# Attention outputs come out transposed: values as the stationary operand, probabilities scaled before their transposition, gates z turned by VectorE's blocks and DRAM

## What is computed

```python
proj = einsum('bsd,de->bse', rms_norm(x), w_in)
qa, ka, va, za, qb, kb, vb, zb, qm, zm, gates = split(proj)
ya = moba_attention(rope(qa), rope(ka), va) * silu(za)      # 8 heads of 128, causal
yb = dilated_mixture(rope(qb), rope(kb), vb) * silu(zb)     # 4 output heads of 128, 3 groups each
ym = memory_attention(qm, mk, mv) * silu(zm)                # 4 heads of 256, over 256 memory rows
g_a, g_b, g_m = split(sigmoid(gates))
merged = g_a * (ya @ w_proj_a) + g_b * (yb @ w_proj_b) + g_m * (ym @ w_proj_m)
x = x + merged @ w_out
```

## Time and profile before

| | |
|---|---|
| runs | 2193.51, 2194.4 and 2196.37 us; median 2194.4 |
| profiled execution | span 2190.4 us from the first to the last instruction; the profile gives no other time for it |
| busy | PE 99%, PEld 82%, DVE 60%, ACT 47%, POOL 7% of the span |
| DMA | mean busy share 0.69, 214 GB/s |
| units | 192 to 731 us of the span |

### The profile page before, as it was taken

The page is one execution under the profiler, slowest core; times in us unless marked ns, Lnnn a source line. Parts: engine busy times, 40 slices in busy tenths (PEclk is TensorE's granted clock), DMA queues, the critical chain, the costliest instruction groups (busy, mean ns, idle before and its releaser), DMA issues.

```text
span 2190.4 us, 25672 instructions
## 1 busy us (share of the span) xinstructions
PE 2177.8 (99%) x9870; PEld 1806.4 (82%) x9870; DVE 1323.6 (60%) x1608; ACT 1029.2 (47%) x1241; POOL 154.3 (7%) x260
## 2 busy tenths in 40 slices
PE   9999999999999999999999999999999999999998
PEld 7788888888888888888888888888888888888887
DVE  5865656676455646545676878665555555554444
ACT  6544444444444444444545666454444444444443
POOL 0010101011000000000111100120001000100000
PEclk9999999999999999999999999999999999999999
DMA  8676656577754657668878756687777777776654
GB/s 302 206 234 176 203 172 208 184 231 238 206 163 149 209 180 229 198 206 285 260 240 284 230 183 200 196 267 230 219 211 225 216 211 212 226 229 203 193 193 154
DMA packets 229731, 468.89 MB, mean 214 GB/s; under 512 B 16632, under 2 KB 16896, under 8 KB 228736
## 3 DMA queue, kind: packets, MB, share of 16 engines
q1 hardware_dynamic: 212128, 409.00, 60.4%
q0 software_dynamic: 17056, 57.69, 8.7%
q10 hardware_dynamic: 448, 0.86, 0.1%
HBM read 439.69 MB, written 27.79 MB: 213 GB/s over the span
## 4 chain that ended last, share of the span: by engine, by line
PE 97%; DVE 2%; DMA 0%; ACT 0%; issue 0%; ACTq 0%; DVEq 0%
PE ps L1549 31%; PE ps L1551 31%; PE ps L1550 31%; PE ps L1448 1%; PE ps L1470 1%; DVE w_lo L916 1%; DVE ps L1266 1%; PE ps L1417 1%; PE ps L1459 0%; DMA raw<-in_w_in 0%; PE ps L1582 0%; PE ps L1583 0%; PE ps L1581 0%; PE ps L1487 0%; PE ps L1519 0%
## 5 line engine op out<-in xcount | busy, mean ns | idle before, releaser
L916 DVE TENSOR_TENSOR w_lo<-raw,w_hi 128x1024 fp32r<-128x1024 f32 (+1 forms) x776 | 931.8, 1211 | 730.4 <-ACT w_hi L605 729.2
L605 ACT ACTIVATE w_hi<-raw 128x1024 fp32r<-128x1024 f32 (+1 forms) x776 | 811.2, 1050 | 910.9 <-PE ps L1551 836.5
L1549 PE MATMUL ps<-w_hi,xT_hi 128*128 128x512 f32 x1088 | 429.8, 395 | 0.0
L1551 PE MATMUL ps<-w_hi,xT_lo 128*128 128x512 f32 x1088 | 424.1, 390 | 0.0
L1550 PE MATMUL ps<-w_lo,xT_hi 128*128 128x512 f32 x1088 | 423.6, 389 | 0.0
L1549 PE MATMUL ps<-w_hi,u2T_hi 128*128 128x512 f32 x704 | 273.9, 389 | 0.0
L1550 PE MATMUL ps<-w_lo,u2T_hi 128*128 128x512 f32 x704 | 273.9, 389 | 0.0
L1551 PE MATMUL ps<-w_hi,u2T_lo 128*128 128x512 f32 x704 | 273.9, 389 | 0.0
L1551 PEld LDWEIGHTS ps<-w_hi,xT_lo 128*128 128x128 f32 x1088 | 204.2, 188 | 43.2
L1550 PEld LDWEIGHTS ps<-w_lo,xT_hi 128*128 128x128 f32 x1088 | 204.5, 188 | 41.0
L1549 PEld LDWEIGHTS ps<-w_hi,xT_hi 128*128 128x128 f32 x1088 | 204.4, 188 | 41.1 <-issue 0.6
(11 more groups left out here) (260 smaller groups left out, 2288.4 us busy)
## 6 DMA issues: line engine op xcount, KB each, us to landing
raw<-in_w_in SPq DMA_DIRECT2D x368, 512.0 KB, 4.4
raw<-in_w_ffn_gate SPq DMA_DIRECT2D x88, 512.0 KB, 4.4
raw<-in_w_ffn_up SPq DMA_DIRECT2D x88, 512.0 KB, 4.6
raw<-in_w_ffn_down SPq DMA_DIRECT2D x88, 512.0 KB, 4.7
raw<-in_w_out SPq DMA_DIRECT2D x64, 512.0 KB, 5.8
bounce<-tmp POOLq DMA_DIRECT2D x45, 512.0 KB, 3.4
stage<-bounce POOLq DMA_DIRECT2D x140, 128.0 KB, 5.2
raw<-in_w_mem_kv SPq DMA_DIRECT2D x32, 512.0 KB, 5.3
```

What stands on the lines that cost most here:

```text
L605: nc.scalar.activation(w_hi[:, s, 0:per], raw[:, s, 0:per], ACT.Copy).then_inc(hi_ready, 1)
L916: nc.vector.tensor_tensor(w_lo[:, s, 0:per], raw[:, s, 0:per], w_hi[:, s, 0:per].bitcast(F32), ALU.subtract)\
L1549: nc.tensor.matmul(bank(2 * par + t), x_hi, w_hi[:, s, k], start=first, stop=False)
L1551: ins = nc.tensor.matmul(bank(2 * par + t), x_lo, w_hi[:, s, k], start=False, stop=last)
```

## The change

Every unit's output now comes out of TensorE already transposed:
- `unit_values` has the values as the stationary operand and the turned probabilities moving. As the tokens are now columns of the output, the factor of a token (reciprocal of its sum times the norm's factor) can't be applied to it there, so a new step of VectorE, `unit_scale`, applies it to the exponentials in `scores` before they are turned. `unit_turn` waits for it (`u_scaled`) and stands behind chunk 3 in place of 2.
- The transposes of `y_tok` are gone. `unit_y` is now VectorE's: one product of the output in PSUM with the gate z. It, `unit_hi` and `unit_lo` run in the tile behind the unit's (behind splits 4 and 5), and the parts are made from `y_tok` in place of PSUM.
- The gates z must then be transposed too (`zmT`, `zaT`, `zbT`): the new kind of post `siluT` writes the tanh and the product into `stage`, turns 32x32 blocks and takes a trip through DRAM, five of them. The numbers of all later trips go up by five. The tile of zb comes ahead of those of vb.
- `unit_scores` takes the blocks of keys of one query block in one matmul of up to 256 columns. Each unit's probabilities are copied by one instruction.
- The steps are now hooks at a chunk (`place`), run last in their chunk. The dilated units start behind chunk 4 of tiles 21 to 24, and these tiles no longer count as tiles with a unit; the tiles 4 to 15 still do.

The core of the diff:

```diff
+        def units_in_tiles():
+            out_ = [(4 + n, 0, mem_unit(n)) for n in range(4)]
+            out_ += [(8 + n, 0, moba_unit(n)) for n in range(8)]
+            return out_ + [(21 + n, 4, dil_unit(n)) for n in range(4)]
...
             def unit_scores(unit):
-                u = w.n["u"]
-                if u:
-                    pe.wait_ge(u_lo, u)
...
-                    for (qs, ks, _), kt in unit["blocks"][t]:
+                    for qs, ks, _ in [src for src, kt in blocks if kt == 0]:
...
-                            ins = nc.tensor.matmul(ps[:, o:o + P], qT[:, qc, t * P:(t + 1) * P], kT[:, kc, kt * P:(kt + 1) * P],
+                            ins = nc.tensor.matmul(ps[:, o:o + kts * P], qT[:, qc, t * P:(t + 1) * P], kT[:, kc, 0:kts * P],
...
             def unit_turn(unit):
-                pe.wait_ge(u_exp, w("u", 1))
+                pe.wait_ge(u_scaled, unit["n"] + 1)
...
             def unit_values(unit):
-                pe.wait_ge(u_pTc, w("u", 1))
+                pe.wait_ge(u_probs, unit["n"] + 1)
+                if unit["n"]:
+                    pe.wait_ge(u_y, unit["n"])
...
+                for d in range(unit["width"] // P):
+                    for n, ((_, _, v), kt, p0, a, b) in enumerate(unit["values"]):
+                        o = unit["o_at"] + d * S
+                        ins = nc.tensor.matmul(ps[:, o + a:o + b], v(kt)[:, d * P:(d + 1) * P], probsT[:, p0:p0 + b - a],
...
-            def unit_y(unit):
-                pe.wait_ge(u_y, w("u", 1))
-                transposes(lambda t, c: y_tok[:, t, c * P:(c + 1) * P], unit["y_at"], unit["width"] // P).then_inc(u_yT, 1)
...
+                place(tiles, "pe_hooks", i, o, lambda unit=unit: unit_scores(unit))
+                place(tiles, "pe_hooks", i, o + 3, lambda unit=unit: unit_turn(unit))
+                place(tiles, "pe_hooks", i, o + (7 if o else 6), lambda unit=unit: unit_values(unit))
...
+            def unit_probs(unit):
+                act.wait_ge(u_turned, unit["n"] + 1)
...
+                place(tiles, "act_hooks", i, o + 4, lambda unit=unit: unit_exp(unit))
+                place(tiles, "act_hooks", i, o + 6, lambda unit=unit: unit_probs(unit))
+                place(tiles, "act_hooks", i, o + 13, lambda unit=unit: unit_hi(unit))
...
-            def unit_norm(unit):
-                dve.wait_ge(u_exp, w("u", 1))
+            def unit_scale(unit):
+                dve.wait_ge(u_exp, unit["n"] + 1)
                 link(nc.vector.reciprocal(rinv, rowsum))
                 link(nc.vector.tensor_tensor(rinv, rinv, R["x"]["r"], ALU.mult))
...
+                    a, n = sb_at(unit, t)
+                    ins = nc.vector.tensor_scalar(scores[:, a:a + n], scores[:, a:a + n], rinv[:, t:t + 1], None, ALU.mult)
+                ins.then_inc(u_scaled, 1)
...
+            def unit_y(unit):
+                dve.wait_ge(b_used, unit["z_turned"])
+                dve.wait_ge(u_out, unit["n"] + 1)
...
+                nc.vector.tensor_tensor(y_tok[:, 0:n], ps[:, o:o + n * S].rearrange("p (c s) -> p c s", s=S), unit["zT"],
+                                        ALU.mult).then_inc(u_y, 1)
...
+                if kind[0] == "siluT":
+                    dve.wait_ge(acc_free[par], w(f"a{par}", 1))
...
-                    if unit and unit_chunk(tile, h) == 4:
-                        unit_mask(unit)
                     if h == pos(tile, tile.get("post_at", 5 if unit else 4 if prev and prev["post"][0] == "res" and prev["post"][3] == "u" else 3)):
                         post(prev, h + 1)
...
                     for f in dict(hooks).get(h, ()):
                         f()
-                if unit and unit_chunk(tile, h) == 7:
-                    unit_norm(unit)
-                    unit_lo(unit)
...
+                place(tiles, "dve_hooks", i, o + 4, lambda unit=unit: unit_mask(unit))
+                place(tiles, "dve_hooks", i, o + 5, lambda unit=unit: unit_scale(unit))
+                place(tiles, "dve_hooks", i, o + 12, lambda unit=unit: unit_y(unit))
+                place(tiles, "dve_hooks", i, o + 13, lambda unit=unit: unit_lo(unit))
```

More of the change, by code:

```diff
@@ L396, in tiles_out @@
             three, four = res_tiles(w_out, "m", x1, 1, what="u")
-            return cut_pair([one, two, far(three, 20), far(four, 21)], 19)
+            return cut_pair([one, two, far(three, 25), far(four, 26)], 24)
         def merge_last(n):
@@ L408, in late_in @@
                 return 2
-            return 9 if len(chunks(tile)) > 9 else 3 if late and (late[0][1] or late[0][0][0] in ("res", "turn") or late[0][0][0] == "rope" and late[0][0][-1] == "late") else 1
+            return 9 if len(chunks(tile)) > 9 else 3 if late and (late[0][1] or late[0][0][0] in ("res", "turn", "siluT") or late[0][0][0] == "rope" and late[0][0][-1] == "late") else 1
         def ffn_last(n):
@@ L434, in tiles_out2 @@
             three, four = res_tiles(w_out2, "y2", h2, 1, what="u2")
-            one, two, three, four = far(one, None), far(two, 31), far(three, 32), far(four, 33)
+            one, two, three, four = far(one, None), far(two, 36), far(three, 37), far(four, 38)
             return [cut(one, 0, 0, 6, True), cut(two, 1, 0, 6, False), cut(one, 0, 6, 7, False), cut(two, 1, 6, 7, False),
@@ new lines, in unit_turn @@
+                for b, k in enumerate(unit["order"]):
+                    o = unit["p_at"] + k * P
+                    ins = nc.tensor.transpose(ps[:, o:o + P], scores[:, b * P:(b + 1) * P], ident)
+                ins.then_inc(u_turned, 1)
+            def unit_values(unit):
+                pe.wait_ge(u_probs, unit["n"] + 1)
+                if unit["n"]:
+                    pe.wait_ge(u_y, unit["n"])
+                if unit["n"] == 3 * QUAD:
+                    pe.wait_ge(acc_free[1], w("a1"))
+                for d in range(unit["width"] // P):
+                    for n, ((_, _, v), kt, p0, a, b) in enumerate(unit["values"]):
+                        o = unit["o_at"] + d * S
+                        ins = nc.tensor.matmul(ps[:, o + a:o + b], v(kt)[:, d * P:(d + 1) * P], probsT[:, p0:p0 + b - a],
+                                               start=n == 0, stop=n == len(unit["values"]) - 1)
@@ L1553, in run @@
                     w.step("g")
-                    if unit and unit_chunk(tile, h) in at_:
-                        (unit_scores, unit_turn, unit_values, unit_y)[at_.index(unit_chunk(tile, h))](unit)
                     if "ret" in tile and h == 0:
```

194 lines of the change are left out of this document (83 added, 111 removed).

## The result

The changed kernel takes 2248.1 us (median of 4 runs, 2245.4 to 2253.8) against 2194.0 for the kernel before on the same chip: a ratio of 1.0253, with a 95% interval of 1.0241 to 1.0266. That is 54 us slower; the forecast was 2234 in a range of 2217 to 2256.

What follows compares the result with a forecast made beforehand. TensorE, busy 99% of the span at 2.4 GHz, was taken as the bound. Waits of 45.4 us less 5.7 us of removed work and waits gave +39.7 us on the 2194.4 median: 2234 us, range 2217 to 2256.

Steps and rivals of the forecast that it cites:

- The waits: TensorE at unit_turn waits for VectorE's unit_scale, queued behind post, unit_y and unit_lo: 15 waits, 45.4 us in all.
- The work removed: On TensorE, y_tok transposes and short waits go and wider matmuls save time: 5.7 us less (5 to 7.5).
- The clock: TensorE's granted clock: a 2.1 us wait left it at the upper level, so no time was added for a fall.
- The forecast's own case: TensorE waits at the turns with the clock up: 2234 us, own range 2217 to 2243, chance 79%.
- the rival's 2256: TensorE's clock falls in eight waits over 3 us, one chunk each at the lower level: +22 us, 2256; chance 10%.
- Two of the signs: In the changed kernel's profile: TensorE's busy time should fall by 5 us; a granted clock leaving its level refutes the forecast.
- What lies beside: Gate z trips through DRAM, POOL's queue, ScalarE's extra copies and raw loads: all covered, adding nothing.
- six chunks or 16 us: ScalarE takes a gate z trip's result that long after the block transposes, against 8.6 us of landings and issues between.
- The three chunks (8.2 us): If a DRAM trip were late and ScalarE's next split waited, TensorE would still have this much matmul work in hand.
- No waits: VectorE's post is through before TensorE reaches the turn, only the transposes are gone: 2189, faster; chance 6%.
- A second wait per tile: ScalarE's late split 7 or VectorE's late split 6 stops TensorE again, 1 to 2 us in twelve tiles: near 2250; 5%.
- Part of the waits only: unit_y, unit_lo and scalings covered or cheaper, 0.7 to 1.4 us off twelve sums: 2217 to 2225; no separate chance given.

Runs made afterwards that it cites:

- the kernel without stops: Changed kernel with post at chunk 3, turn at chunk 5, unit_y and unit_lo behind mask and scaling, dilated units' turn one chunk later: 2185.3 us, ratio 0.9966.
- the two combined edits: Changed kernel with the post at chunk 3 and the memory and MoBA units' turn at chunk 5: 2190.0 us, ratio 0.999.

## Why the prediction came out as it did

**The waits: right, place by place.** The order that it rests on, the hooks last in their chunk and the post in front of them, stands in VectorE's timeline above. Between starts (idle time and 0.16) against the sums: MoBA units under a rotation 4.95 each, 5.0 predicted; memory units under one 3.9, 4.0 predicted; under a gate z 0.8, 3.0 and 2.5, where 0.6, 3.1 and 2.6 were predicted; dilated 0.7 and three of 1.4, as predicted; tile 7 none, as predicted. Only tile 11 is off, 0.4 for 1.1. In all 44.0 for 45.4. The unseen term, scaling of 128 columns, was taken as 0.55 for the pair from the rows of `h2`, and measured 0.55.

**The work removed: a little small.** 5.7 was taken in a range of 5 to 7.5; the difference above gives 6.8, the kernel without stops 5.5 of busy time and 7.8 in the medians. Its parts, the transposes of `y_tok`, the short waits and the wider matmuls, were not measured one by one.

**The clock: the step that failed.** The forecast's own case ended at 2243, and 2248.1 lies above it; the stated range holds it only because its upper end was drawn at the rival's 2256. Two of the signs that the prediction itself named say the same: the granted clock left its level, and TensorE's busy time rose by 14.0 us where it was to fall by 5. The paragraph on the clock left the term at zero, because the longest stop of before, 2.1 us, showed no fall, and put the fall into a rival of 10%: 2.72 us in each of eight stops, +22, "2256". It came with the forecast's own waits: nine falls, 18.0 us, 16.4 given back in the medians when eight of the stops were filled. The price per fall was 2.0 in the mean, not 2.72, since the stretch at the lower level has about 9 slow matmuls and not 12. The fault was not the size. A consequence of the forecast's waits was listed beside them as another case, when 4 to 5 us of standing still were certain in that case and only their effect was open. Nor could have shown a fall at one stop: a slice there is 55 us long, and the page of the kernel with the hooks ahead of the post has a 9 in every slice although slow matmuls follow five of its stops. Windows of a few microseconds show it (the last section has them for the stop of before; the reading was right there). Taken at the rival's own price, the sum would have been 45.4 - 5.7 + 22 = 61.7; with the measured one 45.4 - 5.7 + 18 = 57.7, against 55.2.

The Trainium skill, "TensorE: Matmul & The Clock Gate", Part 1, says that an array that idles is gated down to 1.2 GHz and recovers by activity; the trace agrees, with 0.50 granted from 350 to 354 us and 1.00 from 358. It was named in the prediction and given one chance in ten, on the strength of one stop that was less than half as long as those to come.

**What lies beside: right here, with the help of the waits.** In the changed kernel no copy of ScalarE waits for the new trips: from the write at 350.24 (the start of the DMA instruction on POOL) to the copy of `qaT` at 366.36, a rotation's trip on the same schedule, there are 16.1 us, the 16 of the prediction. But part of those is TensorE standing still. Where the stops were taken away with the post left late, ScalarE reached that copy 8.4 us behind the write (340.21 to 348.65) and waited. It is mostly the trips of the rotations that were late then; of the new ones `zaT` waited 1.8 us. The claim "six chunks or 16 us" took chunks at TensorE's pace, and VectorE and ScalarE go through a backlog of splits at more than twice that. The three chunks (8.2 us) that TensorE was to have in hand behind a late trip failed there too: the mask, the exponentials and the scaling stand behind the late split in their queues, and a copy that came 4.82 us late made the turn stop for 4.00.

**The rivals.** No waits: wrong for this kernel, as said, and its 2189 is about what the two combined edits reach. A second wait per tile: in the changed kernel TensorE waits for `w_lo` 3.8 us in all, so it does not happen. Part of the waits only: 44.0 of 45.4 us came, so no.

## What to carry to other kernels

A wait that is added to an in-order queue is priced by all that stands ahead of the releaser in its engine's queue, a rotation included, and that sum can be made to a few tenths of a microsecond from a timeline of the kernel before. To it belongs the time that TensorE runs slowly once it starts again; if the forecast holds stops longer than any seen at the upper clock, that price goes into the forecast and not beside it. Whether a stop cost the clock is read from windows of a few microseconds around it, since the page's slices are too long to show one. And a stop hides what else is late: before moving a producer back to make room, look at who needs what it sends through DRAM; of the places tried here, only moving the post forward and the consumer back, both at once, cost nothing.

## What was not expected of the hardware

In the changed kernel the clock of TensorE fell in all nine stops of 2.33 us and more. In the kernel with the early post the same happened at two stops of 2.14 us. With the turn two chunks later, even a stop of 1.63 us with another of 0.59 close behind it was followed by slow matmuls (TensorE's timeline of that kernel):

```profile
487.20 0.55 PE L1469 MATMUL ps<-consts,scores 128*128 128x128 f32 x3 [1.63 <-DVE scores L984]
488.34 0.80 PE L1555 MATMUL ps<-w_hi,xT_hi 128*128 128x512 f32 x1 [0.59 <-DVE w_lo L922]
488.93 0.63 PE L1556 MATMUL ps<-w_lo,xT_hi 128*128 128x512 f32 x1
489.35 0.63 PE L1557 MATMUL ps<-w_hi,xT_lo 128*128 128x512 f32 x1
```

With the early post, on the other hand, one of five stops of 3.2 us under a rotation left the clock up, and the matmuls behind it start every 0.23 us (TensorE's timeline of that kernel):

```profile
449.10 0.55 PE L1469 MATMUL ps<-consts,scores 128*128 128x128 f32 x3 [3.21 <-DVE scores L984]
...
449.72 0.39 PE L1556 MATMUL ps<-w_lo,xT_hi 128*128 128x512 f32 x1
449.94 0.39 PE L1557 MATMUL ps<-w_hi,xT_lo 128*128 128x512 f32 x1
```

In the kernel before, a stop of 1.71 us (2.1 for the loader) left the clock at its upper level too (a window of it, the stop among it, and one behind it, columns as above):

```profile
99.00:101.00 2.00, 0.29 (x2) 0.16 (x2) 2.00 (x4) 1.62 (x3) 0.00 (x0) 1.00 0.06 21
101.00:104.00 3.00, 3.00 (x14) 2.44 (x15) 3.00 (x5) 0.00 (x0) 0.00 (x0) 1.00 0.63 190
```

So the length of a single stop did not decide it in these runs; what else does was not tried.
